# A hybrid gating and attention layer on one core: where the second half of a normed row's transposes stands in TensorE's order

## The chip, the cores and the metric

The kernel runs on one core of a Trainium2 chip. The metric is device time in microseconds (us) of one execution; lower is better. The engines have short names in the profile: PE is TensorE (matmuls; PEld are its weight loads), DVE is VectorE, ACT is ScalarE, POOL is GpSimd, SP is SyncE, which issues most of the DMAs.

## The reference, cut to what matters

One layer on x of 1024 rows by 1024 columns, all in float32:

```python
h = rms_norm(x, mix_norm_g)
u_a, v_a, q, k, v = split(h @ w_in)
y_a = rms_norm(spatial_gating(u_a, v_a, ...), group_norm_g[:D_A])
y_b = rms_norm(window_sink_attention(q, k, v, sinks, rel_bias), group_norm_g[D_A:])
x = x + concatenate([y_a, y_b], axis=-1) @ w_out
h = rms_norm(x, ffn_norm_g)
x = x + (silu(h @ w_gate) * (h @ w_up)) @ w_down
return rms_norm(x, final_norm_g)
```

The attention takes, for each chunk of 64 queries, 128 keys and 8 heads: logits plus bias, softmax with a sink term, times v. The change lies in the part from there through the product with w_out to the norm and transposition of the sum for the feed-forward part.

## The kernel before

The 1024 rows are eight tiles of 128, here called rows r = 0 to 7 (T = 8, HT = 4). Matmuls are made exact enough by a split: each operand is a high part (a rounded copy, written by ScalarE) and a low part (what is left, by VectorE), and `split_mm` issues three matmuls, high by high, high by low, low by high (lines 859 to 861). There is no scheduler: the order on every engine is written out by hand, engine by engine, and the engines meet through counting semaphores (`wait_ge`, `then_inc`). An engine takes its instructions strictly in the written order, so whatever stands behind a waiting instruction waits too.

The part of concern is one loop, `for r in range(T)`, that stands once in each engine's program. It is a software pipeline: in iteration r, the attention of row r+1 (and its softmax for row r+2), the product with w_out of rows r and r+1, and the norm and transposes of row r-1 run side by side. Eight banks of PSUM hold the results: 0 to 2 the output units in turn, 3 and 4 logits, 5 the transposed probabilities, 6 the attention output, 7 the transposes of the normed rows.

PE's steps in iteration r, for r = 1 to 6, in order:

- `probs_T(r+1, 0)`: four 128x128 transposes of the softmax S of row r+1, first chunk (line 1043). It waits for `pn_ready`, VectorE's normalised probabilities (`normal_probs`, line 2026).
- `out_unit(r+1, 0)`: 12 matmuls of 512 columns, the first product of row r+1 with w_out (lines 859 to 861).
- `probs_T(r+1, 1)`, and `yb_rows(r)`: one transpose of the summed squares of the attention output (line 1061), which VectorE totals in `yb_totals(r)` (line 2034).
- `out_unit(r+1, 1)`; `h2_transposed(r-1, 0)`, four transposes of the first half of the normed row `x2n` (line 1125); `values(r+1)` (line 1054); `logits(r+3)` (line 1031), up to r = 4.
- `out_unit(r, 2)`; **`h2_transposed(r-1, 1)`**, the second half; `out_unit(r, 3)`.

A group of four transposes is called a block below.

What follows a block of a normed row is `h2_split` on ScalarE (two copies out of bank 7 for rows under 4, lines 1520 and 1521; one for the others, line 1524) and `h2_lo` on VectorE: one subtraction for rows under 4 (line 2073); for the second half of rows 4 and 5 three, T2, T3 and T4 (lines 2082, 2091, 2086). The next half may go into bank 7 only when VectorE has read the one before it (`h2_ready`).

Three more steps are tied to it. ScalarE's `x2_square(r-1)` (line 1511) writes its squares over `x2n`, so it waits until the transposes of the row before are done (`h2_T`). GpSimd turns the sum into a root (lines 649 and 651), VectorE's `norm_x2(r-1)` (line 2066) writes the normed row. ScalarE's `probabilities(r+2)` (line 1457, eight exponentials) stand behind `h2_split(r-1, 0)`, and `yb_square(r+1)` (line 1488), which GpSimd halves and sums (lines 769 and 773), behind `h2_split(r-1, 1)`. The low parts of the first feed-forward weights, `weight_lo(0, "P1", m)` (line 2116), stand at the end of VectorE's iteration 5.

Of the kernel before, what the change touches and what calls it, by code (L numbers as in the profile page):

```python
# [24 lines left out]
def hybrid_trunk_layer(nc, x, xT, mix_gT, w_in, sgu_ln_g, sgu_ln_b, sgu_w, sgu_b, sinks, rel_bias,  # L25
# [277 lines left out]
    with ExitStack() as ctx:  # L303
# [551 lines left out]
        def _(pe):  # L855
# [179 lines left out]
            def probs_T(r, ci):  # L1035
                pe.wait_ge(pn_ready, r + 1)
                if r == 0 and ci == 0:
                    pe.wait_ge(c_summed, added_at("P3", 2))
                if ci == 1:
                    pe.wait_ge(pT_ready, 2 * r + 1)  # L1040
                for g in range(KV):
                    for tp in range(2):
                        last = nc.tensor.transpose(ps[:, 5, (2 * g + tp) * P:(2 * g + tp + 1) * P], S[:, g, ci, tp, :], ident[:])  # L1043
                last.then_inc(p_T, 1)
# [40 lines left out]
            def out_unit(r, n):  # L1085
                u = out_at(r, n) - 1
                h = n % 2
                if u >= 3:
                    pe.wait_ge(out_added, u - 2)
                else:  # L1090
                    pe.wait_ge(c_out, corner_at("P4", u))
                if n < 2:
                    if u == 0:
                        pe.wait_ge(wo_split, HA)
                    if r % HT == 0:
                        pe.wait_ge(ya_ready, 8 if r else 4)
                    lhs = [ya[:, r, hl] for hl in range(2)]
                    rhs = (woA_hi, woA_lo)
                else:
                    pe.wait_ge(yb_ready, r + 1)  # L1100
                    lhs = [yb[r % 2][:, hl] for hl in range(2)]
                    rhs = (woB_hi, woB_lo)
                cs = slice(h * C, (h + 1) * C)
                for k in range(4):
                    if n == 2 and r == 0:
                        pe.wait_ge(wo_split, HA + k + 1)
                    last = split_mm(ps[:, u % 3, :], (lhs[0][:, k, :], lhs[1][:, k, :]), (rhs[0][:, k, cs], rhs[1][:, k, cs]), k == 0, k == 3)
                last.then_inc(out_done, 1)
# [27 lines left out]
            for r in range(T):  # L1136
                if 0 < r < T - 1:
                    probs_T(r + 1, 0)
                    out_unit(r + 1, 0)
                    probs_T(r + 1, 1)  # L1140
                    yb_rows(r)
                if r + 1 < T:
                    out_unit(r + 1, 1)
                    if r:
                        h2_transposed(r - 1, 0)
                    values(r + 1)
                    if r + 3 < T:
                        logits(r + 3)
                    if r == 0:
                        ya_totals(1)  # L1150
                out_unit(r, 2)
                if 0 < r < T - 1:
                    h2_transposed(r - 1, 1)
                if r == T - 2:
                    yb_rows(r + 1)
                out_unit(r, 3)
# [83 lines left out]
        def _(act_e):  # L1240
# [266 lines left out]
            def x2_square(r):  # L1507
                act_e.wait_ge(out_added, out_at(r, 3))
                if r and r < T - 1:
                    act_e.wait_ge(h2_T, 2 * r)  # L1510
                actv((x2n if r < T - 1 else x2_sq_last)[:], xr[r % 3][:], ACT.Square, accum_out=ssq2[:, r:r + 1]).then_inc(x2_sq, 1)
# [66 lines left out]
            for r in range(T):  # L1578
                if r + 1 < T:
                    probs_to_sbuf(r + 1, 0)  # L1580
                if r == 0:
                    woB_piece(3)
                if r:
                    x2_square(r - 1)
                if r + 1 < T:
                    probs_to_sbuf(r + 1, 1)
                    if r:
                        h2_split(r - 1, 0)
                exps = probabilities(r + 2) if r + 2 < T else None
                if exps:  # L1590
                    next(exps)
                if r + 1 < T:
                    yb_to_sbuf(r + 1)
                if exps:
                    next(exps)
                if r and r + 1 < T:
                    h2_split(r - 1, 1)
                if r + 2 < T:
                    yb_square(r + 1)
                elif r + 1 < T:  # L1600
                    yb_square_last()
                if r == 0:
                    for g in YA_ROWS[HT:]:
                        ya_hi_rows(g)
                if r == T - 3:
                    weight_hi(0, "P1", 0)
                    weight_hi(0, "P1", 1)
                if r == T - 2:
                    T2_hi(0)
                    T2_hi(1)  # L1610
# [148 lines left out]
        def _(dve):  # L1759
# [282 lines left out]
            def add_out(r, n):  # L2042
                u, h = out_at(r, n) - 1, n % 2
                cs = slice(h * C, (h + 1) * C)
                dve.wait_ge(out_done, u + 1)
                if n == 0:
                    dve.wait_ge(x_in[r % 3], 32 + 16 * (r // 3 + 1))
                    if r % HT == 0:
                        dve.wait_ge(rA_ready, r // HT + 1)
                if n == 2:  # L2050
                    dve.wait_ge(rB_ready, r + 1)
                    dve.wait_ge(out_added, out_at(r, 1))
                scale = (rA if n < 2 else rB)[:, r:r + 1]
                stt(xr[r % 3][:, cs], ps[:, u % 3, :], scale, xr[r % 3][:, cs], ALU.mult, ALU.add).then_inc(out_added, 1)
# [13 lines left out]
            def h2_lo(r, kh):  # L2068
                flat = "p k n -> p (k n)"
                if r < HT:  # L2070
                    dve.wait_ge(combo_raw, 2 * r + kh + 1)
                    hi, lo = ((B11, B21)[kh][:, r, hl].rearrange(flat) for hl in range(2))
                    tt(lo, ps[:, 7, :], hi.bitcast(F32), ALU.subtract).then_inc(h2_ready, 1)
                    return
                t = r - HT
                T1, T4, T2 = (x.rearrange(flat) for x in (T14_raw[:, t, 0], T14_raw[:, t, 1], T23_raw[:, t, 0]))
                dve.wait_ge(combo_raw, 2 * r + kh + 1)
                if kh == 0:
                    tt(T1, ps[:, H2_BANK[r, kh], :], T1, ALU.subtract).then_inc(h2_ready, 1)
                else:  # L2080
                    dve.wait_ge(h2_ready, 2 * r + (r < T - 1))
                    tt(T2, ps[:, H2_BANK[r, kh], :], T1, ALU.subtract).then_inc(T2_raw, 1)
                    if r < T - 2:
                        h2_T3(r)
                    dve.wait_ge(T2_raw, t + 1)
                    tt(T4, T4, T2, ALU.subtract).then_inc(T4_raw, 1)
# [61 lines left out]
            for r in range(T):  # L2148
                if r in (0, 1, T - 2):
                    yb_totals(r)  # L2150
                if r == T - 1:
                    add_out(r, 2)
                if r:
                    norm_x2(r - 1)
                if r + 2 < T:
                    add_bias(r + 2)
                    if r > 1:
                        yb_totals(r)
                    maxima(r + 2)
                if r and r + 1 < T:  # L2160
                    add_out(r + 1, 0)
                if r == 0:
                    for t in range(1, G):
                        woB_piece(t)
                if r + 1 < T:
                    if r:
                        h2_lo(r - 1, 0)
                    add_out(r + 1, 1)
                    if r == 0:
                        normal_probs(2)  # L2170
                    yb_lo(r + 1)
                if r == 0:
                    ya_total_sums(1)
                elif r + 2 < T:
                    normal_probs(r + 2)
                if r < T - 1:
                    add_out(r, 2)
                if r == T - 2:
                    h2_lo(r - 1, 1)
                add_out(r, 3)  # L2180
                if 0 < r < T - 2:
                    h2_lo(r - 1, 1)
                if r == 0:
                    for g in YA_ROWS[HT:]:
                        ya_lo_rows(g)
                if r == T - 2:
                    T2_to_lo(0)
                    T2_to_lo(1)
                if r == T - 3:
                    weight_lo(0, "P1", 0)  # L2190
                    weight_lo(0, "P1", 1)
# [172 lines left out]
```

## Time and profile before

| | |
|---|---|
| median of 3 runs | 918.24 us (918.23 to 919.0) |
| the profiled execution's own time | 919.09 us |
| its span in the trace | 917.3 us |
| PE busy | 909.7 us (99% of the span) |
| VectorE, ScalarE, GpSimd busy | 588.9, 429.6, 390.4 us |
| matmuls | 4229 |
| the loop's iterations 1 to 6 | from about 185.8 to 275.4 us |

The own time holds, besides the span, what lies around it (1.8 us). The busy time of an engine is the sum over its instructions. Instructions are pipelined, so the recorded length of one may be more than its share of the engine: a matmul of 512 columns is recorded with 0.39 us, and the next starts 0.23 us after it. Distances between starts tell more than lengths.

### The profile page before, as it was taken

The page shows a single profiled execution, that of the slowest core. Times are in us where ns is not written, and L with a number is a line of the kernel's source. Part 1 is how long each engine was busy: PE and PEld are TensorE (multiplying, and loading weights), DVE is VectorE, ACT ScalarE, POOL GpSimd, SP SyncE. Part 2 cuts the span into 40 slices and gives each one's busy share as a digit, 9 for nine tenths or more (in the row PEclk, how much of TensorE's full clock was granted, in tenths as well). Part 3 has the DMA queues.
Part 4 walks back from the last instruction along what each step waited for, and adds up shares of the span by engine and source line. Part 5 has one row for each costly group of instructions (what it writes and reads, how often), then busy time and mean ns, then how long its engine had stood idle before and what let it go on. Part 6 is the DMA issues. An engine that isn't in the chain of part 4 may idle for free.

```text
span 917.3 us, 11969 instructions
## 1 busy us (share of the span) xinstructions
PE 909.7 (99%) x4229; PEld 750.0 (82%) x4229; DVE 588.9 (64%) x785; ACT 429.6 (47%) x835; POOL 390.4 (43%) x387
## 2 busy tenths in 40 slices
PE   9999999999999999999999999999999999999997
PEld 7888888787878888888888888888888888888885
DVE  5759879986779787464453653736547676544754
ACT  6747547856556543243333333333334454444451
POOL 1559732331244379557485574855754000000021
PEclk9999999999999999999999999999999999999999
DMA  9797453211242372744727437264366996656543
GB/s 330 235 267 232 115 161 105 80 70 70 92 138 88 97 220 69 232 136 134 228 68 233 138 126 227 76 226 146 121 223 248 372 368 192 201 187 203 185 138 138
DMA packets 151487, 158.56 MB, mean 173 GB/s; under 512 B 27576, under 2 KB 109060, under 8 KB 151428
## 3 DMA queue, kind: packets, MB, share of 16 engines
q1 hardware_dynamic: 150756, 157.40, 53.0%
q8 instruction: 34, 0.56, 0.3%
q10 hardware_dynamic: 672, 0.40, 0.1%
q14 instruction: 25, 0.20, 0.1%
HBM read 117.26 MB, written 40.50 MB: 172 GB/s over the span
## 4 chain that ended last, share of the span: by engine, by line
PE 98%; issue 1%; ACT 0%; POOL 0%; DVE 0%; POOLq 0%; ACTq 0%
PE ps L859 31%; PE ps L861 31%; PE ps L860 31%; PE ps L1031 1%; PE ps L1054 1%; PE ps L1043 1%; PE ps L979 1%; PE ps L1125 1%; PE ps L883 0%; PE ps L892 0%; PE ps L895 0%; PE ps L898 0%; PE ps L1000 0%; PE ps L990 0%; PE ps L1061 0%
## 5 line engine op out<-in xcount | busy, mean ns | idle before, releaser
L2116 DVE TENSOR_TENSOR P_lo<-P_raw,P_hi 128x512 fp32r<-128x512 f32 x132 | 119.5, 921 | 83.2 <-ACT P_hi L1554 78.8
L859 PE MATMUL ps<-T_hi,P_hi 128*128 128x512 f32 x352 | 136.9, 389 | 0.0
L860 PE MATMUL ps<-T_lo,P_hi 128*128 128x512 f32 x352 | 136.9, 389 | 0.0
L861 PE MATMUL ps<-T_hi,P_lo 128*128 128x512 f32 x352 | 136.9, 389 | 0.0
L801 POOL TENSOR_TENSOR wd<-wd 128x256 f32<-128x256 f32 x88 | 80.9, 919 | 93.6 <-DMA wd<-in_w_down 88.4
L859 PE MATMUL ps<-rb_hi,ra_hi 128*128 128x512 f32 x308 | 119.8, 389 | 0.0
L860 PE MATMUL ps<-rb_lo,ra_hi 128*128 128x512 f32 x308 | 119.8, 389 | 0.0
L861 PE MATMUL ps<-rb_hi,ra_lo 128*128 128x512 f32 x308 | 119.8, 389 | 0.0
L1668 ACT ACTIVATE ra_hi<-ra 128x512 fp32r<-128x512 f32 x77 | 48.6, 631 | 98.8 <-DMA rb<-w_down_T 61.0
L649 POOL TENSOR_SCALAR late<-late 128x1 f32<-128x1 f32 x12 | 6.0, 503 | 191.7 <-ACT junk L1736 178.1
L2225 DVE TENSOR_TENSOR ra_lo<-ra,ra_hi 128x512 fp32r<-128x512 f32 x77 | 55.7, 723 | 36.4 <-ACT ra_hi L1668 36.0
L860 PEld LDWEIGHTS ps<-T_lo,P_hi 128*128 128x128 f32 x352 | 66.1, 188 | 13.8
L861 PEld LDWEIGHTS ps<-T_hi,P_lo 128*128 128x128 f32 x352 | 66.1, 188 | 13.7
L859 PEld LDWEIGHTS ps<-T_hi,P_hi 128*128 128x128 f32 x352 | 66.1, 188 | 13.7
L1554 ACT ACTIVATE P_hi<-P_raw 128x512 fp32r<-128x512 f32 x132 | 76.5, 620 | 0.0
L1659 ACT ACTIVATE G<-G 128x512 f32<-128x512 f32 x33 | 20.9, 633 | 106.7 <-DVE G L2205 106.6
L859 PE MATMUL ps<-B,P_hi 128*128 128x512 f32 x176 | 68.7, 390 | 0.0
L861 PE MATMUL ps<-B,P_lo 128*128 128x512 f32 x176 | 68.5, 389 | 0.0
L860 PE MATMUL ps<-B,P_hi 128*128 128x512 f32 x176 | 68.5, 389 | 0.0
L859 PEld LDWEIGHTS ps<-rb_hi,ra_hi 128*128 128x128 f32 x308 | 57.8, 188 | 12.1
L861 PEld LDWEIGHTS ps<-rb_hi,ra_lo 128*128 128x128 f32 x308 | 57.8, 188 | 12.1
L860 PEld LDWEIGHTS ps<-rb_lo,ra_hi 128*128 128x128 f32 x308 | 57.8, 188 | 11.8
(286 smaller groups left out, 2018.0 us busy)
## 6 DMA issues: line engine op xcount, KB each, us to landing
wd<-in_w_down SPq DMA_DIRECT2D x44, 256.0 KB, 3.3
w_down_T<-wd SPq DMA_DIRECT2D x22, 512.0 KB, 5.0
ra<-act_S SPq DMA_DIRECT2D x44, 256.0 KB, 2.7
rb<-w_down_T SPq DMA_DIRECT2D x44, 256.0 KB, 3.0
act_S<-Q SPq DMA_DIRECT2D x33, 256.0 KB, 3.7
ra<-act_A SPq DMA_DIRECT2D x33, 256.0 KB, 4.4
rb<-in_w_down SPq DMA_DIRECT2D x33, 256.0 KB, 5.0
P_raw<-in_w_gate SPq DMA_DIRECT2D x22, 256.0 KB, 3.7
```

The source lines that it names most:

```text
L801: nc.gpsimd.tensor_tensor(wd[:, d, :], wd[:, x, :], wd[:, y, :], ALU.subtract).then_inc(wd_summed, 1)
L859: mm(dst, lhs[0], rhs[0], start=start, stop=False, skip_group_check=onto)
L860: mm(dst, lhs[0], rhs[1], start=False, stop=False, skip_group_check=onto)
L861: return mm(dst, lhs[1], rhs[0], start=False, stop=stop, skip_group_check=onto)
L979: last = mm(ps[:, MIX_BANK[m % 2], t * P:(t + 1) * P], vn[:, h, HT * half + t], sgu_wT[:, h, :], start=True, stop=True)
L1031: last = mm(ps[:, 3 + g, (2 * ci + tp) * P:(2 * ci + tp + 1) * P], q, kT[rows, c * CH:c * CH + WIN], start=True, stop=True)
L1043: last = nc.tensor.transpose(ps[:, 5, (2 * g + tp) * P:(2 * g + tp + 1) * P], S[:, g, ci, tp, :], ident[:])
L1554: actv(w_h[p, m][:], src[:], ACT.Copy).then_inc(w_hi_ready, 1)
L1659: actv(g[:], g[:], ACT.Silu).then_inc(silu_done, 1)
L1668: actv(ra_hi[n][:], ra[n][:], ACT.Copy).then_inc(step_hi, 1)
L2116: tt(w_l[p, m][:], src[:], w_h[p, m][:].bitcast(F32), ALU.subtract).then_inc(w_split, 1)
L2225: tt(ra_lo[n][:], ra[n][:], ra_hi[n][:].bitcast(F32), ALU.subtract)
```

## The change

The block `h2_transposed(r, 1)` of rows 0 to 4 leaves its place between units (r+1, 2) and (r+1, 3) of iteration r+1, and stands in iteration r+2 behind `probs_T`'s first block. ScalarE's `h2_split(r, 1)` goes from ahead of `yb_square` to behind the next iteration's `x2_square`. VectorE's `h2_lo(r, 1)` is written at the head of the next iteration instead of at the end of its own. Row 5's second half stays (the `r == T - 2` lines), as do rows 6 and 7. SP's and GpSimd's programs are the same.

```diff
@@ tensor
                 if 0 < r < T - 1:
                     probs_T(r + 1, 0)
+                    if r > 1:
+                        h2_transposed(r - 2, 1)
                     out_unit(r + 1, 0)
                     probs_T(r + 1, 1)
                     yb_rows(r)
...
                 out_unit(r, 2)
-                if 0 < r < T - 1:
+                if r == T - 2:
                     h2_transposed(r - 1, 1)
@@ scalar
                 if r:
                     x2_square(r - 1)
+                if 1 < r < T - 1:
+                    h2_split(r - 2, 1)
                 if r + 1 < T:
                     probs_to_sbuf(r + 1, 1)
...
-                if r and r + 1 < T:
+                if r == T - 2:
                     h2_split(r - 1, 1)
@@ vector
                 if r == T - 1:
                     add_out(r, 2)
+                if 1 < r < T - 1:
+                    h2_lo(r - 2, 1)
                 if r:
                     norm_x2(r - 1)
...
                 add_out(r, 3)
-                if 0 < r < T - 2:
-                    h2_lo(r - 1, 1)
```

TensorE, iterations 1 and 2, the piece of the difference for row 0 (woB with yb are units (1,2) and (1,3), woA with ya is unit (3,0); the first rows are the end of unit (1,2)):

```order
 L860 MATMUL ps<-woB_lo_169,yb1_161 128x512
 L861 MATMUL ps<-woB_hi_168,yb1_161 128x512
-L1125 MATMUL ps<-ident_84,x2n_177 128x128 [waits h2_ready,x2n_ready]
-L1125 MATMUL ps<-ident_84,x2n_177 128x128 x3
 L859 MATMUL ps<-woB_hi_168,yb1_161 128x512 [waits yb_ready,out_added]
 L860 MATMUL ps<-woB_lo_169,yb1_161 128x512
...
 L1043 MATMUL ps<-ident_84,S_158 128x128 [waits pn_ready]
 L1043 MATMUL ps<-ident_84,S_158 128x128 x3
+L1125 MATMUL ps<-ident_84,x2n_177 128x128 [waits h2_ready,x2n_ready]
+L1125 MATMUL ps<-ident_84,x2n_177 128x128 x3
 L859 MATMUL ps<-woA_hi_166,ya_165 128x512 [waits out_added]
```

The four transposes now follow the four of the probabilities, and units (1,2) and (1,3) stand one behind the other. There are five such pieces, one for each of rows 0 to 4.

ScalarE, from the end of iteration 1 into iteration 2, before (L1462 is the end of the exponentials, L1520 and L1521 the copies of a half, L1488 the square of yb, L1511 the square of x2):

```order
L1462 ACTIVATE small<-small 128x8 [waits sinkd_ready]
L1520 ACTIVATE B_181<-ps 128x512 [waits ya_ready,h2_T]
L1521 ACTIVATE T_raw<-ps 128x512
L1488 ACTIVATE yb_sq<-yb_raw 128x512 [waits yb_summed,ybraw_ready]
L1469 ACTIVATE pT<-ps 128x512 [waits pv_done,p_T]
L1511 ACTIVATE x2n,late<-xr_175 128x1024 [waits h2_T,out_added]
L1469 ACTIVATE pT<-ps 128x512 [waits pv_done,p_T]
```

and now (two line numbers more):

```order
L1464 ACTIVATE small<-small 128x8 [waits sinkd_ready]
L1490 ACTIVATE yb_sq<-yb_raw 128x512 [waits yb_summed,ybraw_ready]
L1471 ACTIVATE pT<-ps 128x512 [waits pv_done,p_T]
L1513 ACTIVATE x2n,late<-xr_175 128x1024 [waits h2_T,out_added]
L1522 ACTIVATE B_181<-ps 128x512 [waits ya_ready,h2_T]
L1523 ACTIVATE T_raw<-ps 128x512
L1471 ACTIVATE pT<-ps 128x512 [waits pv_done,p_T]
```

The square of yb follows the exponentials directly, and the two copies stand behind the square of x2.

VectorE, from the end of iteration 5 into iteration 6, before (L2082, L2091 and L2086 are row 4's T2, T3 and T4, L2116 the low parts of the weights, L2034 the total of yb, L2066 the normed row 5):

```order
L2054 SCALAR_TENSOR_TENSOR xr_176<-ps,small,xr_176 128x512 [waits out_done]
L2082 TENSOR_TENSOR T_raw<-ps,T_raw 128x512 [waits h2_ready,combo_raw]
L2091 TENSOR_TENSOR T_raw<-ps,T_raw 128x512 [waits combo_raw]
L2086 TENSOR_TENSOR T_raw<-T_raw 128x512 [waits T2_raw]
L2116 TENSOR_TENSOR P_lo_207<-P_raw_193,P_hi_221 128x512 [waits w_hi_ready]
L2116 TENSOR_TENSOR P_lo_208<-P_raw_194,P_hi_222 128x512 [waits w_hi_ready]
L2034 TENSOR_REDUCE small<-ps 128x1 [waits yb_T]
L2066 SCALAR_TENSOR_TENSOR x2n<-xr_176,late,ffn_gB 128x1024 [waits rstd2_ready,h2_T]
```

and now (four line numbers more):

```order
L2058 SCALAR_TENSOR_TENSOR xr_176<-ps,small,xr_176 128x512 [waits out_done]
L2120 TENSOR_TENSOR P_lo_207<-P_raw_193,P_hi_221 128x512 [waits w_hi_ready]
L2120 TENSOR_TENSOR P_lo_208<-P_raw_194,P_hi_222 128x512 [waits w_hi_ready]
L2038 TENSOR_REDUCE small<-ps 128x1 [waits yb_T]
L2086 TENSOR_TENSOR T_raw<-ps,T_raw 128x512 [waits h2_ready,combo_raw]
L2095 TENSOR_TENSOR T_raw<-ps,T_raw 128x512 [waits combo_raw]
L2090 TENSOR_TENSOR T_raw<-T_raw 128x512 [waits T2_raw]
L2070 SCALAR_TENSOR_TENSOR x2n<-xr_176,late,ffn_gB 128x1024 [waits rstd2_ready,h2_T]
```

The three subtractions moved behind the total of yb and stand right ahead of the normed row. In the other iterations VectorE's order is the same as before, since the end of one iteration and the head of the next meet there.

## Rows read from the trace of the kernel before

**Rows 1.** The page: busy time by engine, chain by engine.

```profile
PE 909.7 (99%) x4229; PEld 750.0 (82%) x4229; DVE 588.9 (64%) x785; ACT 429.6 (47%) x835; POOL 390.4 (43%) x387
...
PE 98%; issue 1%; ACT 0%; POOL 0%; DVE 0%; POOLq 0%; ACTq 0%
```

**Rows 2.** Busy time by stretch: engines, granted clock, DMA.

```profile
216.20:231.40 15.20, 15.20 (x90) 12.16 (x89) 10.54 (x17) 9.21 (x28) 2.66 (x6) 1.00 0.18 70
```

**Rows 3.** Timeline (start, us, engine, instruction), PE, iteration 3.

```profile
213.05 0.60 PE L1125 MATMUL ps<-ident,x2n 128*128 128x128 f32 x4
216.24 0.60 PE L1043 MATMUL ps<-ident,S 128*128 128x128 f32 x4
```

**Rows 4.** Timeline, PE, iteration 6: adjacent blocks, matmuls behind.

```profile
271.82 0.60 PE L1125 MATMUL ps<-ident,x2n 128*128 128x128 f32 x4
272.26 0.60 PE L1065 MATMUL ps<-ident,yb_raw 128*128 128x128 f32 x4
275.44 0.39 PE L859 MATMUL ps<-woB_hi,yb 128*128 128x512 f32 x1
278.16 0.39 PE L859 MATMUL ps<-woB_hi,yb 128*128 128x512 f32 x1
```

**Rows 5.** Timeline, end of iteration 1: VectorE, PE.

```profile
199.46 1.23 DVE L2026 TENSOR_TENSOR S<-S,small 128x1024 f32<-128x1024 f32 x1
201.01 0.60 PE L1043 MATMUL ps<-ident,S 128*128 128x128 f32 x4
```

**Rows 6.** Timeline, iteration 3: ScalarE, VectorE and PE.

```profile
217.37 1.05 ACT L1511 ACTIVATE x2n<-xr 128x1024 f32<-128x1024 f32 x1
219.52 1.28 DVE L2066 SCALAR_TENSOR_TENSOR x2n<-xr,late,ffn_gB 128x1024 f32<-128x1024 f32 x1 [1.73 <-POOL late L651]
223.40 0.60 ACT L1520 ACTIVATE B<-ps 128x512 fp32r<-128x512 f32 x1 [2.72 <-PE ps L1125]
229.35 1.22 DVE L2026 TENSOR_TENSOR S<-S,small 128x1024 f32<-128x1024 f32 x1
231.46 0.60 PE L1043 MATMUL ps<-ident,S 128*128 128x128 f32 x4
```

**Rows 7.** Timeline, end of iteration 5: VectorE, PE.

```profile
259.32 1.23 DVE L2026 TENSOR_TENSOR S<-S,small 128x1024 f32<-128x1024 f32 x1
260.85 0.60 PE L1043 MATMUL ps<-ident,S 128*128 128x128 f32 x4
```

**Rows 8.** Timeline, iterations 5 and 6: VectorE and PE.

```profile
261.78 0.68 DVE L2082 TENSOR_TENSOR T_raw<-ps,T_raw 128x512 f32<-128x512 f32 x1
263.57 1.29 DVE L2116 TENSOR_TENSOR P_lo<-P_raw,P_hi 128x512 fp32r<-128x512 f32 x2
264.50 0.27 PE L1061 MATMUL ps<-ident,yb_sum 128*128 128x128 f32 x1
264.80 0.29 DVE L2034 TENSOR_REDUCE small<-ps 128x1 f32<-128x128 f32 x1
265.01 1.27 DVE L2066 SCALAR_TENSOR_TENSOR x2n<-xr,late,ffn_gB 128x1024 f32<-128x1024 f32 x1
267.38 0.60 PE L1125 MATMUL ps<-ident,x2n 128*128 128x128 f32 x4
```

**Rows 9.** Timeline, GpSimd and PE's weight loads at 174 us.

```profile
174.12 0.46 POOL L773 TENSOR_TENSOR yb_sum<-yb_sq 128x128 f32<-128x128 f32 x1
174.64 0.14 PEld L1061 LDWEIGHTS ps<-ident,yb_sum 128*128 128x128 f32 x1 [0.25 <-POOL yb_sum L773]
```

**Rows 10.** Timeline, iterations 0 and 3: ScalarE, VectorE, GpSimd.

```profile
182.67 0.62 ACT L1488 ACTIVATE yb_sq<-yb_raw 128x512 f32<-128x512 f32 x1
183.31 1.23 DVE L2026 TENSOR_TENSOR S<-S,small 128x1024 f32<-128x1024 f32 x1
183.36 1.77 POOL L769 TENSOR_TENSOR yb_sq<-yb_sq 128x256 f32<-128x256 f32 x1 [6.81 <-ACT yb_sq L1488]
230.59 0.74 POOL L769 TENSOR_TENSOR yb_sq<-yb_sq 128x256 f32<-128x256 f32 x1 [7.36 <-ACT yb_sq L1488]
```

## The prediction

> **What bounds the kernel now.** I read the page first. PE is busy 99% of the span, and the chain that ended last is PE for 98% of it [rows 1]: no engine holds PE up anywhere that matters, so the kernel is as long as PE's own work. In the stretch of one loop iteration PE is busy for all of its 15.20 us at the full granted clock (1.00), while VectorE works 10.54, ScalarE 9.21 and GpSimd 2.66 us [rows 2]. So a change of order can do two things only: change what PE pays for its instructions, or make PE wait where it does not wait now. The second question is about slack, and slack is read from the timelines: how long before PE's use each operand is ready.
>
> **The change, part by part.** Five blocks of four transposes move (x2n rows 0 to 4, second half). Each stood between units (r,2) and (r,3) of iteration r = 1 to 5 and now stands behind the first probabilities of iteration r+1. Row 5's block stays. The numbers of instructions are unchanged on every engine.
>
> What PE pays. From a lone block's start to the next block's start, with the 12 matmuls between, is 216.24 - 213.05 = 3.19 us [rows 3]. Two blocks of four in a row start 0.44 us apart, and with 12 matmuls behind them they end at 275.44 - 271.82 = 3.62 us; 12 matmuls with no block take 278.16 - 275.44 = 2.72 us [rows 4]. Before, an iteration has two lone blocks with their units here, 2 x 3.19 = 6.38; after, 2.72 + 3.62 = 6.34. Taking a block out gives 0.47 and putting it beside another costs 0.43: **-0.04 us a move, -0.20 in all**. Bounds: 0 (a block costs the same anywhere) and -0.35 (0.07 each, if the last place of rounding in these rows all lies one way).
>
> What can make PE wait. Three places.
>
> (a) End of iteration 1. The block leaves iteration 1 and nothing enters it, so PE comes to the next first probabilities 0.47 us earlier: 201.01 - 0.47 = 200.54. VectorE's normalised probabilities, which these transposes read, start at 199.46 and end at 200.69 [rows 5], and nothing in the change makes them earlier: ScalarE's two copies of the moved half came after the exponentials. PE must wait. How long after a release it starts: GpSimd ended at 174.58 and the waiting weight load began at 174.64 [rows 9], 0.06 later; that load takes 0.14, so the matmul follows 0.06 to 0.20 after the release, and I take 0.10, as PE overlaps load and matmul. The wait is 200.69 + 0.10 - 200.54 = **+0.25 us**.
>
> (b) Iterations 2 to 4. Here the block is added in front and removed behind, and the period stays 15.2. But what hangs on the first half's transposes of row r-1 comes 0.43 later: ScalarE's copy (223.40, which waited for PE [rows 6]), the eight exponentials behind it on ScalarE, and VectorE's probabilities, which end at 229.35 + 1.22 = 230.57. They would end at 231.00, and with the 0.10 PE can start at 231.10; it arrives at 231.46 - 0.04 = 231.42. The slack shrinks from 0.79 to 0.32 and **nothing is lost**. The other new dependence: ScalarE copies the moved half after the square (217.37 + 1.05), two copies of 0.60 that overlap a little, to about 219.5; VectorE's subtraction (0.6) now stands between that and the normed row (219.52 [rows 6]), which starts about 0.6 later, near 220.1, and ends near 221.4. The copy at 223.40 waited for transposes of that normed row which began some 0.6 earlier, so about 1.4 is left. VectorE's next add_bias and maxima slip by the same 0.6, and ScalarE's exponentials, already 0.43 later, hide all but a trace of it. SP's load of x row r+3 waits for the normed row too, but is not used until the next iteration.
>
> (c) End of iteration 5. This iteration has no logits block on PE, so PE comes round sooner, and the probabilities end at 259.32 + 1.23 = 260.55 for a block at 260.85 [rows 7]: slack 0.30 and no more. They come 0.43 later, PE 0.04 earlier: 260.55 + 0.43 + 0.10 - 260.81 = **+0.27 us**.
>
> (d) Iteration 6, the largest. Row 4's subtraction is three VectorE instructions (T2, T3, T4). Now they stand before the low parts of two weights and the total of yb: 263.57 - 261.78 = 1.79 us [rows 8]. After, they stand behind that total and right ahead of the normed row 5. The total waits for PE's one transpose (264.50 + 0.27) and starts at 264.80; it would be 0.43 later, as PE is. From its start: 0.21 to the next instruction, 1.79 for the three, 1.27 for the normed row, 0.10 to PE: 264.80 + 3.37 = 268.17, against PE's use at 267.38, and both sides carry the same 0.43. PE waits **+0.79 us**, where it had 267.38 - 266.28 = 1.10 us of slack. The cover for the three instructions was PE's long unit; it is gone because VectorE's queue holds them behind a wait on PE. Queued behind them are the residual add of unit (7,0) and the subtraction of row 5's first half. Both are due when PE comes to the second half and to unit (6,3), 271.82 and after [rows 4], against about 270.5 when the second is done: over 1 us, and PE's own wait adds to it.
>
> Sum: -0.20 + 0.25 + 0.27 + 0.79 = **+1.11 us**. Against the profiled execution's own 919.09 that is 920.2; the median of the runs is 918.24, 0.85 below it, and I carry the difference over: **919.3**. The release time is used three times, so 0.06 or 0.20 in its place gives 1.0 or 1.4.
>
> One rule is weighed here. The square of yb on ScalarE no longer has the two copies ahead of it, so GpSimd's halving of it comes about when VectorE's probabilities start. The row for this is iteration 0, where nothing stood between the exponentials and the square: square 182.67, VectorE 183.31, GpSimd 183.36; VectorE kept its 1.23 us and GpSimd took 1.77 where it takes 0.74 alone [rows 10]. So I take 0 for VectorE.
>
> The Trainium skill (SBUF — State Buffer, "Who interferes with whom") says a VectorE instruction with two SBUF inputs and a GpSimd instruction that reads SBUF exclude each other, and whoever issues first holds the port for the whole instruction. By that rule, the trace agrees on GpSimd's 1.77; the sum would be as above with VectorE first and as in rival B with GpSimd first.
>
> **The rivals.**
>
> A: no stall to speak of; the three waits are absorbed and only the -0.20 is left: 918.0. For it: PE is never held up in this stretch today. Against: (a) rests on one subtraction of two rows and needs nothing to be later than it is. 10%.
>
> B, slower: GpSimd gets ahead of VectorE at the probabilities. GpSimd's halving then takes its 0.74 and VectorE's 1.23 us start 0.05 + 0.74 = 0.79 later. It decides from a lead of VectorE of 0.05 us [rows 10], which is thin. Price: 0.79 each in iterations 1 and 5, and 0.79 - 0.32 = 0.47 in each of 2, 3 and 4, 2.99 in all: 1.11 + 2.99 = 4.1 and 922.3. Against: five sequences would have to fall the other way than the one that the trace shows. 8%.
>
> C, slower too: the stalls are mine, but larger. If the copies, their waits or a second reader delay the probabilities by 0.3 more in each of the five iterations, (a) and (c) grow by 0.3 each, and the other three by nothing; if also the normed row in iteration 6 is delayed by GpSimd's products from 267.6 on, 0.3 more: 2.0 and 920.2. 15%.
>
> D: the change does not do what it says, for example since a wait on x2n or the bank holds the moved block itself. Its operands (row r-1's normed row, the first half's subtraction) are ready long before (219.52 + 1.28 = 220.80 [rows 6] for a block near 231.9), and bank 7 is then free. The time would be that of the forecast or worse. 2%.
>
> **How the numbers follow.** The forecast (two short waits, one of 0.8 us, a gain of 0.2) has 65%. About 0.2% (1.84 us) is what a measurement of this kernel can tell from no change. The forecast's +1.1 is within it, with bounds of 0.8 to 1.6 from its terms, and a median of few runs moves by some tenths more. Slower by over 0.2%: all of B, most of C, and a twentieth of the forecast: 0.25. Faster by over 0.2% needs -1.84 where the terms can give -0.35: 0.02. Within: 0.73. The range reaches from A (918.0, less 0.1) to just short of B's full price: 917.9 to 921.5.
>
> **What would show it.** In the profile after: PE idle or a late block at three places, before the probabilities' transposes of iterations 2 and 6 (about 0.25 each) and before row 5's first half in iteration 6 (0.8, released by VectorE's normed row); 12 matmuls of units (r,3) in 2.72 us; GpSimd's halving near 1.7 us with VectorE's probabilities still at 1.23. Iterations 3 to 5 should start 15.2 us apart. I am wrong if VectorE's probabilities take 1.8 us or more (B), if PE never waits (A), or if PE's granted clock falls below 1.00 anywhere in this stretch.

## The result and the profile after

Over 22 runs of each, the changed kernel takes 919.65 us (median) and the kernel before 918.36: ratio 1.0013, 95% interval 1.0007 to 1.0019, or +1.3 us with an interval from 0.6 to 1.7. That is slower, and within the 0.2% that I called no change. The forecast was +1.11 (919.3). The 919.3 started from the median of three runs before, 918.24; over the 22 it is 918.36, which is 0.12 of the 0.35 that lie between forecast and median.

The page of the changed kernel, with the rows that answer to [rows 1]:

```profile
span 917.3 us, 11969 instructions
...
PE 909.0 (99%) x4229; PEld 749.5 (82%) x4229; DVE 587.1 (64%) x785; ACT 429.8 (47%) x835; POOL 395.5 (43%) x387
...
PE 97%; issue 1%; ACT 1%; DVE 1%; POOL 0%; POOLq 0%; DVEq 0%; ACTq 0%
```

The span is the same 917.3 us as in the trace before, and the profiled execution's own time is 919.17. That does not contradict the medians. The two executions differ before the loop: iteration 1 begins at 184.86 here and at 185.78 in the trace before, 0.92 us earlier, where the change alters nothing. This start differs from execution to execution (184.49 to 185.92 over the ten kernels of this study), and one span cannot show a microsecond. So I measure inside the trace, between two fixed PE instructions: from the first probabilities' block of iteration 1 to the first matmul of the feed-forward part. Before, that is 280.88 - 185.78 = 95.10 us; after, 280.92 - 184.86 = **96.06**. What lies behind it took 636.4 us in both. The change costs 0.96 us in this stretch, inside the interval of the runs.

The waits of PE's weight loads, by what released them (engine, line waited for: us in total, times, longest). The trace before has neither of these two rows:

```profile
PEld ps L1125 <- DVE x2n L2070: 1.0, 1, 1.0
PEld ps L1043 <- DVE S L2030: 0.9, 2, 0.5
```

The busy times by stretch, for iteration 1, iteration 3 and iteration 6 to the feed-forward part (columns as in [rows 2]):

```profile
184.86:199.79 14.93, 14.92 (x86) 11.64 (x84) 12.70 (x22) 8.37 (x26) 5.71 (x8) 1.00 0.19 71
215.01:230.17 15.16, 15.16 (x90) 12.21 (x89) 10.49 (x18) 9.12 (x28) 3.71 (x7) 1.00 0.19 70
259.64:280.92 21.28, 20.66 (x106) 16.61 (x107) 16.33 (x22) 9.62 (x18) 11.34 (x15) 1.00 0.49 149
```

The granted clock is 1.00 in all three, and over the whole of 180 to 285 us. The last stretch is 21.28 us with PE busy for 20.66: 0.62 us of open idle time. Iteration 3 is full, as before [rows 2].

Each of the three places, and the one where I expected nothing, in the timeline. First the end of iteration 1, which answers to [rows 5]:

```profile
197.78 0.19 ACT L1464 ACTIVATE small<-small 128x8 f32<-128x8 f32 x1
197.88 0.62 ACT L1490 ACTIVATE yb_sq<-yb_raw 128x512 f32<-128x512 f32 x1
198.51 1.22 DVE L2030 TENSOR_TENSOR S<-S,small 128x1024 f32<-128x1024 f32 x1
198.57 1.76 POOL L769 TENSOR_TENSOR yb_sq<-yb_sq 128x256 f32<-128x256 f32 x1 [7.32 <-ACT yb_sq L1490]
199.79 0.42 PEld L1043 LDWEIGHTS ps<-ident,S 128*128 128x128 f32 x4 [0.44 <-DVE S L2030]
199.79 0.66 PE L1043 MATMUL ps<-ident,S 128*128 128x128 f32 x4
```

VectorE's probabilities end at 198.51 + 1.22 = 199.73, and PE's load, which had been idle for 0.44, starts at 199.79. The block is recorded as starting with its load, is 0.66 long in place of 0.60, and the block behind it follows at 200.29, 0.50 later; behind a block that did not wait it is 0.43 to 0.44 (below, iteration 3). So I count the start of a block that waited as 0.06 too early. This is a reading of the records, and no run measures it by itself. GpSimd's halving came 0.06 behind VectorE, took 1.76 and left VectorE's 1.22 untouched, as in iteration 0 [rows 10].

Iteration 3's end, answering to [rows 6]:

```profile
228.53 1.23 DVE L2030 TENSOR_TENSOR S<-S,small 128x1024 f32<-128x1024 f32 x1
230.17 0.60 PE L1043 MATMUL ps<-ident,S 128*128 128x128 f32 x4
230.61 0.60 PE L1125 MATMUL ps<-ident,x2n 128*128 128x128 f32 x4
```

VectorE ends at 229.76, 0.41 us before the block at 230.17; less the 0.10 for the release the slack is 0.31, where I had 0.32. The moved block follows 0.44 later.

Iteration 5's end, answering to [rows 7]:

```profile
258.36 1.23 DVE L2030 TENSOR_TENSOR S<-S,small 128x1024 f32<-128x1024 f32 x1
259.64 0.66 PE L1043 MATMUL ps<-ident,S 128*128 128x128 f32 x4
```

259.59 to 259.64: again PE starts at the release, with a record of 0.66.

Iteration 6, answering to [rows 8]:

```profile
263.76 0.27 PE L1061 MATMUL ps<-ident,yb_sum 128*128 128x128 f32 x1
264.07 0.29 DVE L2038 TENSOR_REDUCE small<-ps 128x1 f32<-128x128 f32 x1 [1.97 <-PE ps L1061]
264.28 0.68 DVE L2086 TENSOR_TENSOR T_raw<-ps,T_raw 128x512 f32<-128x512 f32 x1
264.88 0.68 DVE L2095 TENSOR_TENSOR T_raw<-ps,T_raw 128x512 f32<-128x512 f32 x1
265.47 0.68 DVE L2090 TENSOR_TENSOR T_raw<-T_raw 128x512 f32<-128x512 f32 x1
266.07 1.28 DVE L2070 SCALAR_TENSOR_TENSOR x2n<-xr,late,ffn_gB 128x1024 f32<-128x1024 f32 x1
267.41 0.66 PE L1125 MATMUL ps<-ident,x2n 128*128 128x128 f32 x4 [0.62 <-DVE x2n L2070]
```

The total of yb starts 0.04 after PE's transpose has ended (263.76 + 0.27), the three subtractions take 266.07 - 264.28 = 1.79 up to the next instruction, the normed row ends at 267.35, and PE's block starts at 267.41. Unhindered it would have come 267.38 - 264.50 = 2.88 us after the transpose [rows 8], at 266.64: 0.77 late, or 0.83 with the 0.06 of a block that waited.

### The profile page after: what moved, and what is told of

Its sections match the earlier page's. It is cut to its first block, busy times and chain, and to the rows that moved or that the text cites. A ratio compares the mean times of both kernels' runs of the same rounds, so it can differ in the third digit from the quotient of the medians.

```text
span 917.3 us, 11969 instructions
## 1 busy us (share of the span) xinstructions
PE 909.0 (99%) x4229; PEld 749.5 (82%) x4229; DVE 587.1 (64%) x785; ACT 429.8 (47%) x835; POOL 395.5 (43%) x387
## 4 chain that ended last, share of the span: by engine, by line
PE 97%; issue 1%; ACT 1%; DVE 1%; POOL 0%; POOLq 0%; DVEq 0%; ACTq 0%
PE ps L859 31%; PE ps L861 30%; PE ps L860 30%; PE ps L1031 1%; PE ps L1043 1%; PE ps L1125 1%; PE ps L979 1%; PE ps L1054 1%; PE ps L883 0%; ACT S L1459 0%; PE ps L892 0%; PE ps L895 0%; PE ps L898 0%; PE ps L1000 0%; DVE S L2030 0%
```

## The experiments

All eight are measured by the same stretch. The table gives the lengths of iterations 1 to 5, from first block to first block, then from iteration 6's first block to the feed-forward part; each stretch is read from one profiled execution. The times of the runs stand beside it, and the ratio is to the kernel before on the same chip (its medians beside the experiments were 918.52 and 918.5).

| kernel | 1 | 2 | 3 | 4 | 5 | 6 | stretch | median us | ratio (95%) |
|---|---|---|---|---|---|---|---|---|---|
| before | 15.23 | 15.23 | 15.22 | 15.23 | 14.16 | 20.03 | 95.10 | 918.36 | |
| the change | 14.93 | 15.22 | 15.16 | 15.16 | 14.31 | 21.28 | 96.06 | 919.65 | 1.0013 (1.0007 to 1.0019) |
| row 4 stays | 14.95 | 15.21 | 15.17 | 15.16 | 14.56 | 20.04 | 95.09 | 918.43 | 0.9998 (0.9989 to 1.0008) |
| T2 to T4 ahead | 14.97 | 15.21 | 15.16 | 15.16 | 14.32 | 20.51 | 95.33 | 919.02 | 1.0005 (0.9996 to 1.0015) |
| row 0 stays | 15.23 | 14.75 | 15.16 | 15.16 | 14.33 | 21.32 | 95.95 | 919.27 | 1.0008 (0.9999 to 1.0017) |
| square ahead | 16.04 | 15.95 | 15.96 | 15.95 | 15.57 | 21.30 | 100.77 | 924.5 | 1.0064 (1.0049 to 1.0079) |
| exponentials first | 14.76 | 15.15 | 15.17 | 15.15 | 14.10 | 21.26 | 95.59 | 919.2 | 1.001 (1.0 to 1.0019) |
| the same, and T2 to T4 ahead | 14.76 | 15.15 | 15.17 | 15.15 | 14.10 | 20.41 | 94.74 | 918.25 | 0.9998 (0.9989 to 1.0007) |
| exponentials first, in the kernel before | 15.23 | 15.22 | 15.23 | 15.23 | 14.15 | 20.04 | 95.10 | 918.33 | 0.9997 (0.9988 to 1.0007) |
| rows 1 to 3 only | 15.23 | 14.75 | 15.16 | 15.16 | 14.58 | 19.97 | 94.85 | 918.04 | 0.9997 (0.9988 to 1.0006) |

The intervals of the runs are about 0.9 us wide on each side, so only the verdicts on the change and on the square rest on them; the others rest on the stretch. Where two kernels have the same instructions and no wait, an iteration repeats within 0.02 us (iterations 3 and 4 down the table), the longer last piece within 0.07 (20.03, 20.04, 20.04, 19.97). The runs bear the stretch out as far as they reach: the median less the stretch lies between 823.2 and 823.7 us for all ten kernels.

**Row 4's second half stays where it was.**

```diff
-                    if r > 1:
+                    if 2 <= r < 6:
                         h2_transposed(r - 2, 1)
...
-                if r == T - 2:
+                if 4 < r < T - 1:
                     h2_transposed(r - 1, 1)
```

and the same bounds on `h2_split` and `h2_lo`.

> The changed kernel, but row 4's second half stays in its old place on the three engines; rows 0 to 3 move. Measure: PE's stretch from the first probabilities' block of iteration 1 to the first matmul of the feed-forward part, 95.10 us before and 96.06 with the change. Theory (three waits): this takes away the wait of 0.27 at the end of iteration 5 and the one of 0.79 in iteration 6, and one move of -0.04; left are -0.16 and about +0.2 at the end of iteration 1, so 95.1 to 95.2. Rival (a block put beside another costs PE more by itself, the same at each of the five moves): four fifths of the 0.96, so 95.87.

Measured: 95.09. This is 0.01 under what I expected. Iterations 1 to 4 are those of the change. Iteration 5 has a block in front and keeps its own: 14.56, that is 14.16 and 0.40 for the added block, with no wait; and the last piece is 20.04, as before. A price of 0.2 a move would have left 95.87, and falls.

**Row 4's three subtractions ahead of the total of yb.** Only VectorE's order at the head of iteration 6 differs.

```diff
+                if r == T - 2:
+                    h2_lo(r - 2, 1)
                 if r in (0, 1, T - 2):
                     yb_totals(r)
...
-                if 1 < r < T - 1:
+                if 1 < r < T - 2:
                     h2_lo(r - 2, 1)
```

> The changed kernel, with only VectorE's order at the head of iteration 6 altered: row 4's three subtractions stand ahead of the total of yb instead of behind it. Theory: their operands are there by 262.6, so they end near 264.4, the total starts then, the normed row near 264.6 ends at 265.9, before PE's 266.6; the wait for x2n is gone and the stretch is 96.06 - 0.77 = 95.3. Rival (the three subtractions in themselves are too late in iteration 6, wherever they stand in it): the wait stays at half or more, 95.7 or above.

Measured: 95.33. VectorE and PE in iteration 6:

```profile
263.70 0.69 DVE L2086 TENSOR_TENSOR T_raw<-ps,T_raw 128x512 f32<-128x512 f32 x1 [0.50 <-ACT B_raw L1526]
265.51 0.29 DVE L2038 TENSOR_REDUCE small<-ps 128x1 f32<-128x128 f32 x1
265.71 1.28 DVE L2070 SCALAR_TENSOR_TENSOR x2n<-xr,late,ffn_gB 128x1024 f32<-128x1024 f32 x1
267.76 0.60 PE L1125 MATMUL ps<-ident,x2n 128*128 128x128 f32 x4
```

The subtractions start as soon as ScalarE's copy is there, the total follows them at once, the normed row ends at 266.99, and PE's block at 267.76 has 0.77 us in hand. So the wait in iteration 6 was one of order: the same three instructions, before the wait for PE and not behind it, cost nothing.

**Row 0's second half stays where it was.** The bounds of the three engines start one row later (`if 3 <= r < 7` for the new place, `if 0 < r < 2 or 5 < r < T - 1` for the old).

> The changed kernel, but row 0's second half stays in its old place; rows 1 to 4 move. Theory: the wait at the end of iteration 1 (about 0.2) goes, and does not come back at the end of iteration 2, since there the probabilities have 0.79 us of slack and PE comes only 0.47 earlier; one move of -0.04 less: 95.85 to 95.9. Rival (the first iteration without a block always pays): the wait moves to iteration 2 and the stretch stays at 96.06 to 96.10.

Measured: 95.95; iteration 1 is 15.23 again and iteration 2 is 14.75, that is 0.47 to 0.48 shorter, the whole price of a removed block. VectorE and PE at the end of iteration 2:

```profile
212.82 1.23 DVE L2030 TENSOR_TENSOR S<-S,small 128x1024 f32<-128x1024 f32 x1
214.47 0.60 PE L1043 MATMUL ps<-ident,S 128*128 128x128 f32 x4
```

The probabilities end at 214.05, 0.42 before the block: no wait. The rival (the first iteration without a block always pays) falls. The stretch came out 0.05 to 0.10 above what I expected. Iterations 5 and 6 are at 14.33 and 21.32 where the change has 14.31 and 21.28, with the same instructions. Iterations 1 and 2 together gave 30.15 - 29.98 = 0.17: the wait of 0.23 less 0.07 for the move, which is worth more than the 0.04 that I had taken (see below).

**ScalarE's square ahead of the sink's exponential.** This forces the order of rival B.

```diff
                 last.then_inc(p_ready, 1)
+                if 3 <= r:
+                    yb_square(r - 1)
                 act_e.wait_ge(sinkd_ready, r + 1)
                 actv(sink_e, sink_d, ACT.Exp).then_inc(sinke_ready, 1)
...
-                if r + 2 < T:
+                if r == 0:
                     yb_square(r + 1)
+                elif r + 2 < T:
+                    pass
```

> The changed kernel, with ScalarE's square of yb put ahead of the sink's exponential in iterations 1 to 5, so that GpSimd's halving of it starts ahead of VectorE's probabilities. The square itself makes the probabilities 0.5 us later. Theory with the port held by whoever is first: VectorE waits out the rest of GpSimd's 0.74 as well, its probabilities take 1.4 us in place of 1.23 and end 0.68 later; PE loses 0.68 in iterations 1 and 5 and 0.68 - 0.32 in each of 2, 3 and 4, 2.4 in all, stretch 98.5. Rival (VectorE is not blocked by GpSimd): 1.23 us, 0.5 later, loss 1.5, stretch 97.6. If the slack of iterations 2 to 4 is not the 0.32 that I worked out, the loss there differs from both.

Measured: 100.77, a loss of 4.7 us against the change. Both figures were too low. Iteration 3's end:

```profile
230.35 0.62 ACT L1492 ACTIVATE yb_sq<-yb_raw 128x512 f32<-128x512 f32 x1
230.87 0.19 ACT L1466 ACTIVATE small<-small 128x8 f32<-128x8 f32 x1
231.04 0.73 POOL L769 TENSOR_TENSOR yb_sq<-yb_sq 128x256 f32<-128x256 f32 x1 [5.76 <-ACT yb_sq L1492]
231.85 0.47 POOL L773 TENSOR_TENSOR yb_sum<-yb_sq 128x128 f32<-128x128 f32 x1
231.17 0.64 DVE L2029 TENSOR_TENSOR small<-small 128x8 f32<-128x8 f32 x1 [1.54 <-ACT small L1466]
232.07 1.33 DVE L2034 TENSOR_TENSOR S<-S,small 128x1024 f32<-128x1024 f32 x1
233.46 0.66 PE L1043 MATMUL ps<-ident,S 128*128 128x128 f32 x4 [0.58 <-DVE S L2034]
```

GpSimd's halving starts at 231.04. VectorE's first small sum, 8 columns, which takes 0.17 us otherwise, starts at 231.17 and takes 0.64: it ends at 231.81, 0.04 after GpSimd's 231.77. Then GpSimd's second sum, issued 0.01 after the reciprocal's start, runs beside it, and the probabilities take 1.33 in place of 1.23. That the second sum causes this 0.10 is not shown; up to that sum's recorded end, 232.32, it would be 0.25. From the sink's exponential to the end of the probabilities it is 233.40 - 230.87 = 2.53 us, against 229.76 - 227.79 = 1.97 in the change. With the 0.52 of the square itself the probabilities are 1.08 later. Iterations 3 and 4 lose 15.96 - 15.16 = 0.80 and 15.95 - 15.16 = 0.79, where 1.08 less the slack of 0.31 is 0.77; iteration 2 loses 0.73, and 0.06 more if its early recorded start in the change is counted. Iterations 1 and 5 lose all of it and more (1.11 and 1.26). Of the excess of 0.18 in iteration 5, 0.06 is the early record of its first block, which waits here and not in the change, and 0.10 stands on ScalarE, whose exponentials start 0.59 after the copy ahead of them (257.63 and 257.04) and in the change 0.49 (253.39 and 252.90); what holds them stays open. So the blocking is real (VectorE is not free of GpSimd) and the slack was sized right; what I had wrong is which instruction is blocked. I had looked only at the long one.

**The exponentials and the probabilities first.** ScalarE does the second four exponentials ahead of yb's copy, and VectorE the probabilities ahead of yb's low part, in iterations 1 to 5.

```diff
                 if exps:
                     next(exps)
-                if r + 1 < T:
+                if r == 0:
                     yb_to_sbuf(r + 1)
                 if exps:
                     next(exps)
+                if 0 < r < T - 1:
+                    yb_to_sbuf(r + 1)
...
                     if r == 0:
                         normal_probs(2)
+                    elif r + 2 < T:
+                        normal_probs(r + 2)
                     yb_lo(r + 1)
                 if r == 0:
                     ya_total_sums(1)
-                elif r + 2 < T:
-                    normal_probs(r + 2)
```

On the changed kernel alone:

> The changed kernel, with the exponentials and probabilities ahead of yb's copy and low part only; row 4's subtractions as in the change. Theory: the waits at the end of iterations 1 and 5 go (0.23 and 0.25), the one in iteration 6 stays at 0.76: stretch 95.57, no PE wait released by the probabilities. Rival (those two waits come from something else that is late at the same place): 96.0.

Measured: 95.59. VectorE and PE at the end of iteration 5, and the waits of PE's loads (only the normed row's is left; there is no row for the probabilities):

```profile
256.96 1.23 DVE L2032 TENSOR_TENSOR S<-S,small 128x1024 f32<-128x1024 f32 x1
259.17 0.60 PE L1043 MATMUL ps<-ident,S 128*128 128x128 f32 x4
PEld ps L1125 <- DVE x2n L2072: 1.0, 1, 1.0
```

The probabilities end at 258.19, 0.98 before the block, and iterations 1 and 5 are 14.76 and 14.10. The two waits together were 96.06 - 95.59 = 0.47 us.

On the kernel before, as a control:

> The kernel before, with the exponentials and probabilities ahead of yb's copy and low part. A control: PE never waits there, so nothing on PE can get earlier; stretch 95.10, as before. If this edit by itself gains or costs, it shows here.

Measured: 95.10. By itself the edit moves nothing: slack that PE does not use is worth nothing.

With T2 to T4 ahead as well:

> The changed kernel, with both remedies: row 4's three subtractions ahead of the total of yb, and ScalarE's second four exponentials and VectorE's probabilities ahead of yb's copy to SBUF and its low part. Theory: all three waits are gone and only the price of the moves is left, 96.05 - 0.76 - 0.25 - 0.23 = 94.8 us for the stretch, 0.3 under before; in device time too little to tell from no change. Rival (VectorE's low part of yb, now behind the probabilities, meets GpSimd's halving and pushes the residual adds and the normed row back): a new wait for x2n and a stretch of 95.1 or more.

Measured: 94.74, the shortest of all. VectorE, GpSimd and PE at the end of iteration 3:

```profile
227.70 1.23 DVE L2032 TENSOR_TENSOR S<-S,small 128x1024 f32<-128x1024 f32 x1
228.84 0.69 DVE L2036 TENSOR_TENSOR yb<-yb_raw,yb 128x512 fp32r<-128x512 f32 x1
228.90 1.23 POOL L769 TENSOR_TENSOR yb_sq<-yb_sq 128x256 f32<-128x256 f32 x1 [5.96 <-ACT yb_sq L1490]
230.50 0.60 PE L1043 MATMUL ps<-ident,S 128*128 128x128 f32 x4
```

yb's low part and GpSimd's halving do meet, 0.06 us apart, but GpSimd is second and takes the loss (1.23 for 0.74), and nothing of it reaches PE. The rival falls. In device time the kernel is at 0.9998 of the one before, not to be told from it.

**Rows 1 to 3 only.** The bounds of the first and the third experiment together.

> Only rows 1 to 3 move; rows 0, 4 and 5 stay. Theory: none of the three places is left, three moves at -0.06 each: stretch 95.10 - 0.18 = 94.92. Rival (every run of moves pays at its first and at its last iteration): a wait at the end of iteration 2, stretch above 95.1.

Measured: 94.85, with no wait of PE at either end. It is 0.07 below what I expected; 0.06 of that lies in the last piece (19.97 against 20.03), where the two kernels have the same instructions on PE, so I do not credit it to the moves. It is spread over the whole piece in steps of 0.01 to 0.02. What made that piece shorter stays open.

## Why the prediction was right, step by step

- **The price of a move** (-0.04 each, -0.20 in all). With all waits taken away five moves give 94.74 - 95.10 = -0.36, 0.07 each, at the very end of my bounds. Taking a block out gives 0.47 as I had it; putting it beside another costs 0.38 to 0.42 and not 0.43 (iteration 6: 20.41 against 20.03; iteration 5 with row 4 staying: 14.56, and with rows 1 to 3 only 14.58, against 14.16). I could have read this beforehand. My 3.19 us for a block with its 12 matmuls was a block of the normed row; the added block stands beside one of the probabilities, and from that one to the next block it is 219.45 - 216.24 = 3.21 before and 218.62 - 215.01 = 3.61 after (the first line is of the kernel before, the second of the changed one):

```profile
219.45 0.60 PE L1043 MATMUL ps<-ident,S 128*128 128x128 f32 x4
218.62 0.60 PE L1043 MATMUL ps<-ident,S 128*128 128x128 f32 x4
```

  That is 0.40 for the added block, and 0.07 for the move. This term was mis-sized by 0.16 us, and the sum was to that extent too high.
- **(a), end of iteration 1** (+0.25). 14.93 - 14.76 = 0.17, plus the 0.06 by which a block that waited is recorded early: 0.23.
- **(b), iterations 2 to 4** (nothing, slack 0.32). Nothing, slack 0.31; the experiment with the square spent this slack and paid what lay beyond it, to some 0.02. The normed row starts 218.90 - 215.01 = 3.89 us into iteration 3, where it was 219.52 - 216.24 = 3.28: 0.61 later, as I had it (0.6), and PE does not feel it.
- **(c), end of iteration 5** (+0.27). 14.31 - 14.10 = 0.21, plus 0.06: 0.27. By the whole stretch it is 0.24, what (a) leaves of the 0.47 for both.
- **(d), iteration 6** (+0.79). 0.83 by the timeline, the 0.06 included. Taking the wait away gave 96.06 - 95.33 = 0.73 in one pair of kernels and 95.59 - 94.74 = 0.85 in the other. From the head of iteration 6 to the normed row's block, where the wait ends, it is 7.77 against 7.02 in the one pair and 7.71 against 6.94 in the other: 0.75 and 0.77, or 0.81 and 0.83 with the 0.06. The rest of the 0.12 lies where the kernels of a pair have the same instructions and no wait (0.04 of it in iteration 1, 14.93 against 14.97), and I take it for scatter.
- **The sum.** -0.36 + 0.23 + 0.24 + 0.85 = 0.96 is the measured stretch by construction, since these are differences of the same kernels. With (c) as read from its own iteration and (d) from the timeline against the kernel before it is -0.36 + 0.23 + 0.27 + 0.83 = 0.97, which is a check. My four terms gave 1.11. The runs say 1.3 with an interval that holds both.
- **VectorE ahead of GpSimd** by 0.05 to 0.06 us (rival B). It held in every iteration: the probabilities took 1.22 to 1.23 and GpSimd's halving 1.75 to 1.77, where alone it takes 0.74 [rows 10]. The order decides, as the Trainium skill (SBUF — State Buffer, "Who interferes with whom") has it: whoever is first keeps the port. The case with GpSimd first was forced, and there it was VectorE that waited. My price for the rival (0.79 each) was worked out for the long instruction alone and is not shown by any run.
- **Rival A** (no waits) and **rival C** (larger waits) did not happen; nor did D. The kernel with both remedies is what A described, by other means.

What the change bought, 0.36 us of PE's time, was real. It was lost more than three times over because the moved block had been the cover for two short waits. VectorE's three subtractions, in their old place, had run under PE's long unit; behind the total of yb they made one long wait.

## What to carry to other kernels

When one engine is busy for the whole span, price a move twice: once for what the busy engine pays, and once for every operand that others hand it, by the time between ready and used. A block that leaves an iteration uncovers what was ready just in time there; an instruction that moves behind a wait on another queue inherits that wait, even where it has no part in it. And where two executions differ by a microsecond before the part that was changed, measure between two fixed instructions inside the trace.

## What the runs showed of the hardware that I had not expected

- A VectorE instruction of 8 columns with two inputs from SBUF, 0.17 us alone, took 0.64 beside GpSimd's halving of 256 columns that had started 0.12 to 0.13 earlier, in each of the five iterations of the experiment with the square. It ended 0.02 to 0.04 after the halving's end (231.81 against 231.77), so I read it as a wait for the whole of the other.
- A PE block that waited is recorded with matmul and weight load starting together (199.79) and the group of four 0.66 long, where in the flow the load comes 0.23 ahead (229.94 for the block at 230.17) and the group is 0.60. By the block behind it, distances from such a start are 0.06 us too long.
- Four transposes beside four others cost PE 0.38 to 0.42 us, alone between matmuls 0.47.
